# A hybrid decoder step: the opening of the scan is worked in the state loop, and the memory rows change their weight slots

## The reference, cut to what matters

```python
m = rmsnorm(mem, g_mem)                       # 256 rows
k, v = m @ w_mem_k, m @ w_mem_v
dt = softplus(dt_raw + dt_bias)
acs = cumsum(dt * a)                          # in each chunk of 128 tokens
decay = exp(where(causal, acs[l] - acs[s], -inf))
wgt = (C_l . B_s) * decay * dt[s]
y_diag = wgt @ x                              # within a chunk, per head
states = B^T (exp(acs_end - acs) * dt * x)    # carried from chunk to chunk
y_off = C (h_prev) * exp(acs)
y = y_diag + y_off + x * d_skip
out = concat(pool_out, rmsnorm(y * silu(z))) @ w_out
```

## Time and profile before

| | |
|---|---|
| median of 3 runs | 2381.19 us (2380.41 to 2382.19) |
| the profiled execution | 2378.9 us, its span 2377.2 us |
| mean granted clock of TensorE | 0.991 |
| PE | 2326.0 us busy, 98% of the span |
| DVE | 1241.7 us, 52% |
| ACT | 593.3 us, 25% |
| POOL | 58.6 us, 2% |
| DMA | 169.21 MB, mean 71 GB/s |

### The profile page before, as it was taken

How to read it: one execution, slowest core, us unless ns; L and a number is a source line. 1 busy time by engine, 2 the same in 40 slices (tenths; PEclk the granted TensorE clock), 3 DMA queues, 4 the chain that set the end, 5 groups by cost and what they waited for, 6 DMA issues and landing times.

```text
span 2377.2 us, 37042 instructions
## 1 busy us (share of the span) xinstructions
PE 2326.0 (98%) x14994; PEld 2244.9 (94%) x14994; DVE 1241.7 (52%) x2301; ACT 593.3 (25%) x1020; POOL 58.6 (2%) x100
## 2 busy tenths in 40 slices
PE   7999999999999899999999999999999999999998
PEld 7999999999999899985789988999999999999998
DVE  5544444444445775454867635266444444444445
ACT  6111111111112332234623124141111111111112
POOL 0000000000000000012210000000000000000000
PEclk8999999999999999998999999999999999999999
DMA  4111111111111321056523424311111111111111
GB/s 147 36 54 35 53 35 53 53 41 47 35 53 41 111 55 53 30 155 213 198 78 101 152 90 151 117 54 36 54 35 53 53 52 36 42 46 50 39 36 74
DMA packets 185419, 169.21 MB, mean 71 GB/s; under 512 B 6659, under 2 KB 165137, under 8 KB 185065
## 3 DMA queue, kind: packets, MB, share of 16 engines
q1 hardware_dynamic: 185329, 167.94, 22.6%
HBM read 147.98 MB, written 20.04 MB: 71 GB/s over the span
## 4 chain that ended last, share of the span: by engine, by line
PE 60%; DVE 2%; ACT 1%; issue 1%; DVEq 0%; ACTq 0%
PE bank L2237 17%; PE bank L2238 17%; PE bank L2239 17%; PE bank L2813 1%; PE bank L2825 1%; PE bank L2717 1%; PE bank L2713 1%; PE bank L2845 1%; PE bank L2923 0%; PE bank L2722 0%; PE bank L2834 0%; PE bank L2867 0%; PE bank L2733 0%; PE bank L2657 0%; PE bank L2855 0%
## 5 line engine op out<-in xcount | busy, mean ns | idle before, releaser
L2237 PE MATMUL bank<-h_hi,w_hi 128*128 128x352 f32 x3120 | 1012.6, 325 | 5.2 <-DVE pre L1524 2.2
L2239 PE MATMUL bank<-h_hi,w_lo 128*128 128x352 f32 x3120 | 1001.1, 321 | 0.0
L2238 PE MATMUL bank<-h_lo,w_hi 128*128 128x352 f32 x3120 | 1001.0, 321 | 0.0
L2237 PEld LDWEIGHTS bank<-h_hi,w_hi 128*128 128x128 f32 x3120 | 586.4, 188 | 8.2 <-DVE pre L1524 2.8
L2238 PEld LDWEIGHTS bank<-h_lo,w_hi 128*128 128x128 f32 x3120 | 587.7, 188 | 0.8
L2239 PEld LDWEIGHTS bank<-h_hi,w_lo 128*128 128x128 f32 x3120 | 586.0, 188 | 0.0
L1401 DVE SCALAR_TENSOR_TENSOR x<-bank,x 128x352 f32<-128x352 f32 x528 | 275.8, 523 | 191.4 <-PE bank L2239 191.1
L2237 PE MATMUL bank<-mid_hi,w_hi 128*128 128x352 f32 x1056 | 342.4, 324 | 8.1 <-DVE x L1401 8.1
L2238 PE MATMUL bank<-mid_lo,w_hi 128*128 128x352 f32 x1056 | 339.2, 321 | 0.0
L2239 PE MATMUL bank<-mid_hi,w_lo 128*128 128x352 f32 x1056 | 338.9, 321 | 0.0
L1316 DVE TENSOR_TENSOR w_lo<-w_raw,w_hi 128x1024 fp32r<-128x1024 f32 x190 | 229.3, 1235 | 50.3 <-ACT w_hi L859 48.4
(11 more groups left out here) (334 smaller groups left out, 1474.9 us busy)
## 6 DMA issues: line engine op xcount, KB each, us to landing
w_raw<-in_w_gate_dram SPq DMA_DIRECT2D x44, 512.0 KB, 3.8
w_raw<-in_w_up_dram SPq DMA_DIRECT2D x44, 512.0 KB, 4.5
w_raw<-in_w_down_dram SPq DMA_DIRECT2D x44, 512.0 KB, 4.1
w_raw<-in_w_in_dram SPq DMA_DIRECT2D x18, 512.0 KB, 4.8
x_spill<-x SPq DMA_DIRECT2D x6, 1408.0 KB, 6.2
kring<-in_cache_mem_k_dram SPq DMA_DIRECT2D x8, 1024.0 KB, 5.0
vring<-in_cache_mem_v_dram SPq DMA_DIRECT2D x8, 1024.0 KB, 5.0
dec<-acs_row SPq DMA_DIRECT2D x8, 768.0 KB, 6.1
```

The lines of the kernel that those rows point to most:

```text
L2237: eng.matmul(out, a_hi, b_hi, start=first, stop=False)
L2238: eng.matmul(out, a_hi, b_lo, start=False, stop=False)
L2239: return eng.matmul(out, a_lo, b_hi, start=False, stop=last)
```

## The change

Three things are altered. `mem_hi` and `mem_lo` lie in slots 2 and 3, the keys' and values' units in slots 0, 1, 4 and 5, and the turns and splits of the two memory rows stand later in pairs 7 and 8. The skip diagonals, the first output-weight unit, the first half of chunk 1's decays and the second output-weight unit are worked on ACT in and right behind the state loop, and DVE splits both output weights ahead of the transposed outputs. For that `dec0` and `dec1` change places, and SP loads chunk 1's decay rows ahead of the output weights.

```diff
@@ buffers
-        mem_hi = sb("mem_hi", "WH", 0, [P, KT, NMEM], F32R)
-        mem_lo = sb("mem_lo", "WL", 0, [P, KT, NMEM], F32R)
+        mem_hi = sb("mem_hi", "WH", 8192, [P, KT, NMEM], F32R)
+        mem_lo = sb("mem_lo", "WL", 8192, [P, KT, NMEM], F32R)
-        dec = [sb("dec0", "HH", 10240, [P, HEADS, P]), sb("dec1", "HH", 24576, [P, HEADS, P]),
+        dec = [sb("dec0", "HH", 24576, [P, HEADS, P]), sb("dec1", "HH", 10240, [P, HEADS, P]),
@@ slot_of, wait_slot
-            return 2 + (w - U_KV) % 4 if U_KV <= w < U_OUT else w % 6
+            return (0, 1, 4, 5)[(w - U_KV) % 4] if U_KV <= w < U_OUT else w % 6
-                    eng.wait_ge(kv_used, 16 if k < 2 else 11 + k)
+                    eng.wait_ge(kv_used, (13, 14, 16, 16, 15, 16)[k])
@@ SP
             kv_out(2)
+            eng.wait_ge(s_x[4], 48)
+            eng.wait_ge(yt_ready, 1)
+            eng.wait_ge(s_ktout, 64)
+            dec_load(1)
             for k in range(2):
                 unit(U_OUT + k, wv["w_out"][:, :, k * P:(k + 1) * P])
...
-            eng.wait_ge(s_x[4], 48)
             eng.wait_ge(yo_ready, NB)
-            eng.wait_ge(s_ktout, 64)
-            dec_load(1)
             dec_load(2)
@@ ACT, pairs 7 and 8
-                    if (pair, n) in ((7, 2), (8, 0)):
-                        if n == 2:
-                            eng.wait_ge(r_sq, 11)
-                        mem_split(pair - 7)
-                    if (pair, n) == (8, 1):
+                    if (pair, n) == (8, 0):
+                        eng.wait_ge(p_ready, 48)
+                        eng.wait_ge(r_sq, 11)
+                    if (pair, n) in ((8, 0), (8, 2)):
+                        mem_split(n // 2)
+                    if (pair, n) == (8, 2):
                         hi_pair(U_KV)
@@ ACT, state loop and behind it (decays_half is one half of decays)
+                if b == 6:
+                    eng.wait_ge(acs_c, 2)
+                    eng.wait_ge(s_h0x, 2)
+                    for j in range(YT):
+                        for e in range(2):
+                            half = slice(64 * e, 64 * e + 64)
+                            ins = eng.activation(dsk[half, j, :], ident[half, half], ACT.Copy, scale=dskip[half, j:j + 1])
+                    link(ins)
+                    hi_unit(U_OUT, 0, 0)
+            decays_half(1, 0)
+            hi_unit(U_OUT, 1, 0)
             eng.wait_ge(yo_ready, NB)
             eng.activation(yb[:, :], bank[2][:, 0:3 * HD], ACT.Copy).then_inc(yc_done, 1)
             kv_evict(3)
-            hi_pair(U_OUT)
...
-            (the waits and the loop that wrote dsk)
             take_b(1)
-            eng.wait_ge(acs_c, 2)
-            decays(1)
+            decays_half(1, 1)
@@ DVE, pairs 7 and 8
                     evict_in(7, n, mm)
-                    if (n, mm) == (2, 0):
-                        mem_low(0)
...
                     evict_in(8, n, mm)
-                if n == 0:
-                    mem_low(1)
-                if n == 1:
+                    if (n, mm) in ((0, 0), (2, 0)):
+                        mem_low(n // 2)
+                if n == 2:
                     w_pair(U_KV)
@@ DVE, behind the state loop
+            w_pair(U_OUT)
             eng.wait_ge(yt_ready, 2)
...
-                if i == 9:
-                    w_pair(U_OUT)
@@ PE, pairs 7 and 8
-                    if n and pair == 7:
-                        mem_turn(n - 1)
+                    if (pair, n) == (7, 2):
+                        mem_turn(0)
+                    if (pair, n) == (8, 1):
+                        mem_turn(1)
```

More of the change, by code:

```diff
@@ L1123, in _, with decays_half @@
                 hi_unit(U_KV, j, 0)
+            def decays_half(q_, g):
+                d_ = dec[(q_ - 1) % 3]
+                if g == 0:
+                    eng.wait_ge(s_x[(q_ - 1) % 3], 32 + 16 * ((q_ - 1) // 3 + 1))
+                for h in range(HG * g, HG * g + HG):
+                    ins = eng.activation(d_[:, h, :], d_[:, h, :], ACT.Relu, bias=acs[:, q_ - 1, h:h + 1], scale=-1.0)
+                link(ins)
+                eng.activation(d_[:, HG * g:HG * g + HG, :], d_[:, HG * g:HG * g + HG, :], ACT.Exp, scale=-1.0).then_inc(e_done, 1)
             for b in range(NB):
@@ L1136, in _ @@
             kv_evict(3)
-            hi_pair(U_OUT)
             def decays(q_):
[L1141 to L1147, removed]
+                decays_half(q_, 0)
+                decays_half(q_, 1)
             def take_b(q_):
```

## The result

The changed kernel takes 2388.89 us (median of 7, 2385.28 to 2396.36) against 2380.93 us (7 runs, 2378.52 to 2382.85): ratio 1.0035, 95% interval 1.0019 to 1.0051, so by the ratio 8.3 us slower (4.5 to 12.1); the medians are 8.0 us apart. A second set on another chip gave 1.0030 (1.0018 to 1.0042).

What follows compares the result with a forecast made beforehand. PE, busy 98% of the span, was taken as the bound. +6.5 + 0.3 - 1.2 = +5.6 us took the profiled 2378.9 to 2384.5 us; with 2.3 for the median, 2386.8 us, range 2380.5 to 2390.0.

Steps and rivals of the forecast that it cites:

- rival C: Key units and scan: gaps bring uncovered half-clock work, the scan gains nothing; +8 to +9 us, 2389.7 us, chance 0.18.
- A: The forecast itself, memory rows and scan together: +5.6 us (+3.5 to +7.5), 2386.8 us, chance 0.52.
- Term one: Memory rows: the second key weight's load goes out later, delaying the `dt` chain and PE; +6.5 us, bounds 5.5 to 8.5.
- the five I had: Key units up to the `dt` chain's end: PE waits of 2.1, 0.8, 2.0, 0.8 and 0.7 us.
- What is not covered, 0.3 us: Key units: half-clock work behind PE's gaps that later waits do not cover, +0.3 us.
- Term two: Scan opening: `cea` limits the gain to 2.2 us, less 1.0 for the clock; -1.2 us, bounds -5.8 and +0.5.
- the exponentials' gain: Scan start: PE's 2.0 us wait on the exponentials of `dec` goes; 5.8 us open at scale_c(2) without the `cea` limit.
- Rival B: Scan opening: pays in full if `cea` lands before 1124.5; +1.0 us in all, 2382.2 us, chance 0.20.
- rival D: State loop: paced by its own loads, it takes in the rows' delay; -5 us, 2376.2 us, chance 0.10.
- chunk 1 would start 4 us sooner: Scan: PE, no longer waiting for btok, may start chunk 1 at about 1120, 4 us sooner.
- The step that costs nothing: State loop and scan: the b = 7 copy 0.5 us late, the earlier decay load, new buffer order and slots cost nothing.

Runs made afterwards that it cites:

- e1_rows_alone: The kernel before with only the memory rows' slots, turns and splits as in the change: 2391.74 us, ratio 1.0044.
- e3_rows_sooner: The changed kernel with the second memory row turned, split and released one step sooner: 2381.11 us, ratio 1.0004 to the kernel before.
- e0_after_again: The changed kernel run once more, unaltered, for its spread and a second profile: 2387.84 us, ratio 1.0030 to the kernel before.
- e2_scan_alone: The kernel before with only the scan opening's part, the output weights split where they were: 2380.74 us, ratio 0.9996.
- e4: e3_rows_sooner with chunk 2's `cea` load issued ahead of chunk 3's decay rows and the last four state outputs: 2377.84 us, ratio 0.9996 to the kernel before.

## Why the prediction was right, point by point

**Right, in sign and nearly in size.** Forecast +5.6 us and 2386.8 us, measured +8.3 (4.5 to 12.1) and 2388.9; by the table, 6.8 for the rows, 0.8 for the state loop and -0.3 for the scan (means of 89.7 and 89.97) make 7.3 up to hT. The size is nearer to rival C's: +8.3 lies above the bounds that I gave my own sum (+3.5 to +7.5) and within C's +8 to +9, and 2388.9 is 2.1 us from A's 2386.8 and 0.8 from C's 2389.7. The interval (4.5 to 12.1) holds both. What the profiles show lies between the two: A's place and cost for the rows, and nearly C's "the scan gains nothing".

**Term one, the memory rows: right, place and size.** I had the load out at 1029.6 and `w_hi` until 1034.65; it was 1030.9 and 1035.8, in a profile whose pooling ended 1.3 us later. The chain of dt was to start 6.7 us later; from the pooling it is 6.7 to 6.8 in each of three profiles. The waits on split key weights were there, by PE's timeline of the changed kernel:

```profile
1033.85 0.50 PE L2243 MATMUL bank<-w_hi,mem_hi 128*128 128x512 f32 x1 [1.99 <-DVE w_lo L1325]
```
```profile
1042.02 0.50 PE L2243 MATMUL bank<-w_hi,mem_hi 128*128 128x512 f32 x1 [0.79 <-DVE w_lo L1325]
...
1045.38 0.50 PE L2243 MATMUL bank<-w_hi,mem_hi 128*128 128x512 f32 x1 [0.32 <-DVE w_lo L1325]
...
1048.95 0.46 PE L2581 MATMUL bank<-dta,upper 128*128 128x96 f32 x2 [0.52 <-DVEq L1765]
```

1.99, 0.79 and 0.32 us on `w_lo` and 0.52 on the chain of dt are named, less than the five I had (2.1 to 0.7). No wait is named before the second key unit: the first one ran at half clock behind the gap of 1.99 (granted clock 0.78 in 1033 to 1037 and 0.80 in 1037 to 1041, where PE had nothing sooner to do), and so filled it. That the half-clock work would fall in time in which PE waits anyway was as I had expected. e1_rows_alone shows the term in time, 1.0044, and e3_rows_sooner takes all but 0.8 us of it away.

**"What is not covered, 0.3 us": too small.** MEMSET to yb is 79.6 rather than 78.8 us, and a half-clock stretch behind a gap may be long: it cost 7.9 us in one run of three profiled. Rival C had the mechanism, and had its place wrong: not at the key units, but in the state loop, behind a gap that the kernel before has too. That it makes the spread of the change's runs is likely and not shown; one profile has it.

**Term two, the scan: right for the reason given, the size too large.** scale_c(2) came 17.9, 17.6 and 17.7 us behind yb, 19.5 before: 1.6 to 1.9 us gained, where I had 2.2. The load of `cea` landed 17.5 to 17.8 us behind yb, 19.3 to 19.6 before: 1.5 to 2.1 us sooner, where I had 2.4. The wait on `cea` was 2.8, 2.9 and 2.4 us, I had 3.5. PE was to stand idle for some 3 us before chunk 2 and then to work at half clock. It went so in e0_after_again, with 4.7 us of waiting and 0.50 in 1139 to 1145 us, and there the scan was some 0.6 us longer than before, not shorter. In the other two profiles the time is filled by work at half clock ahead of chunk 2, and the scan is some 0.6 us shorter. Together -0.3 us by the profiles, where I had -1.2, and e2_scan_alone measures the part (without the output weights) at -1.0 us (-3.6 to +1.9). With the queue in another order (e4) the exponentials' gain comes out in the profile. Rival B, the full gain, is refuted by the wait; rival D, by the state loop, which took in nothing. My statement that chunk 1 would start 4 us sooner was right in one profile of the change (4.5 us sooner against yb) and wrong in two (1.8 and 1.7). In those two the work ahead of it ran at half clock, at 0.50 from 1131 to 1138 and from 1124 to 1140; in the third there was a short stretch alone, 0.57 in 1125 to 1129, and then 1.00 until the wait was over.

**The step that costs nothing:** output weights in the loop, 0.5 us late at b = 7, and the first decay load: no wait names them. For the slots it holds but for the 0.8 us that e3_rows_sooner keeps; where these arise is not shown.

## What to carry to other kernels

When a tile moves to another slot, follow its source as well as its place: here the slot was free, but the row kept a raw buffer 11 us longer, and the next load, ACT, DVE's chain and PE queued up behind it in that order. Before an engine's wait is taken away, look for the load that lands just before its next step; one that lands 0.2 us ahead in a full DMA queue will be the next wait. Here its place in the issue order took that wait away. On an engine that is 98% busy, small orders (one eviction behind one weight, 3.6 us, 0.7 to 6.7) are worth as much as a rebuilt opening.

## What was not expected of the hardware

A half-clock stretch behind a wait of PE is not of a fixed length, and need not come at all. Behind the same 2.44 us wait at b = 3 there was none in e4_cea_first, some 3 us in three profiles of the kernel before, some 7 us in two of the change and some 20 us in one. At the scan opening of the change it took some 17 us in two profiles, and some 3 us in the third with another of some 7 us behind the wait. In the last 750 us, with the same instructions and the same two waits, there were none, one or two, at 1.6 us each. So the work from the last softmax row to the end took from 887.2 to 891.3 us over the fourteen profiles, 887.2 to 889.6 in one kernel. A profile's span alone can't show a gain of 3 us. A stretch between two events can, if the granted clock in it is read beside it.
